# Modulation vectors of a two-block transformer: weights made the stationary operand, in plain f32

## What is computed

```python
mod = jax.nn.silu(c) @ w_mod[l] + b_mod[l]
sh1, sc1, gt1, sh2, sc2, gt2 = jnp.split(mod[:, None, :], N_MOD, axis=-1)
mod_c = jax.nn.silu(c_ctx) @ w_mod[l] + b_mod[l]
h_lat = modulate_2(x, norm1_g[l], sh1, sc1)
h_ctx = modulate_2(ctx, norm1_g[l], csh1, csc1)
```

## Time and profile before

| | us |
|---|---|
| median of 3 runs | 4677.69 |
| lowest, highest run | 4676.04, 4678.01 |
| span of the profiled execution, first to last instruction | 4676.2 |
| from the first load of `w_mod` to the end of the last bias addition, `mod1` | 8.68 to 95.62 |
| the same for `mod2` | 2651.00 to 2735.62 |
| TensorE matmuls, share of the span | 74% |
| TensorE weight loads, share of the span | 59% |
| mean granted TensorE clock, share of 2.4 GHz | 0.878 |

### The profile page before, as it was taken

How to read it: one execution, slowest core, us unless ns; L and a number is a source line. 1 busy time by engine, 2 the same in 40 slices (tenths; PEclk the granted TensorE clock), 3 DMA queues, 4 the chain that set the end, 5 groups by cost and what they waited for, 6 DMA issues and landing times. The chain is left out here.

```text
span 4676.2 us, 54928 instructions
## 1 busy us (share of the span) xinstructions
PE 3468.8 (74%) x18716; PEld 2774.4 (59%) x18716; DVE 2909.6 (62%) x4362; ACT 1528.0 (33%) x1968; POOL 1362.9 (29%) x512
## 2 busy tenths in 40 slices
PE   6683767876777777777777676877676987877968
PEld 3473537865565666666656345757355865766856
DVE  5224647773799998999999645349747823144441
ACT  5110421112355555555555431112013521212121
POOL 0020000001255555655555202115320033333423
PEclk9895888967899999999999888887788998988989
DMA  6110000000587887887887531000010022222322
GB/s 250 50 61 9 5 25 1 1 15 23 214 296 270 299 295 273 297 294 273 298 296 281 190 117 50 35 26 1 0 45 7 1 72 72 73 71 77 98 66 74
DMA packets 136745, 573.07 MB, mean 123 GB/s; under 512 B 12977, under 2 KB 17457, under 8 KB 103729
## 3 DMA queue, kind: packets, MB, share of 16 engines
q1 hardware_dynamic: 136528, 570.21, 34.4%
HBM read 568.07 MB, written 2.10 MB: 122 GB/s over the span
## 5 line engine op out<-in xcount | busy, mean ns | idle before, releaser
L1841 POOL TENSOR_TENSOR ex_d_low<-ex_d,ex_d_high 128x1024 fp32r<-128x1024 f32 x256 | 800.3, 3126 | 724.8 <-ACT ex_d_high L1823 724.8
L1770 PE MATMUL psum<-ex_gu_high,ex_xe 128*128 128x256 f32 x2048 | 560.0, 308 | 371.6 <-DVE ex_gu_low L1876 367.3
L1770 PEld LDWEIGHTS psum<-ex_gu_high,ex_xe 128*128 128x128 f32 x2048 | 417.2, 204 | 497.5 <-DVE ex_gu_low L1876 424.2
L1876 DVE TENSOR_TENSOR ex_gu_low<-ex_gu,ex_gu_high 128x2048 fp32r<-128x2048 f32 x256 | 620.5, 2424 | 63.0 <-ACT ex_gu_high L1812 51.3
L1770 PE MATMUL psum<-ex_gu_low,ex_xe 128*128 128x256 f32 x2048 | 535.0, 295 | 0.0
L1812 ACT CAST ex_gu_high<-ex_gu 128x2048 fp32r<-128x2048 f32 x256 | 486.7, 1901 | 9.7 <-DMA ex_gu<-in_w_gate_up 5.8
L1770 PEld LDWEIGHTS psum<-ex_gu_low,ex_xe 128*128 128x128 f32 x2048 | 418.7, 204 | 0.9
L1892 DVE CAST ex_hT<-ex_hid 128x64 fp32r<-128x64 f32 x256 | 400.8, 1565 | 8.9
L466 POOL TENSOR_TENSOR out_w_low<-out_w,out_w_high 128x1024 fp32r<-128x1024 f32 x16 | 39.3, 2463 | 786.6 <-ACT out_w_high L431 786.6
L1823 ACT CAST ex_d_high<-ex_d 128x1024 fp32r<-128x1024 f32 x256 | 266.1, 1040 | 2.7 <-PE psum L1794 2.4
L1794 PE MATMUL psum<-ex_d_high,ex_hT 128*128 128x512 f32 x512 | 229.7, 449 | 12.4 <-POOL ex_d_low L1841 9.8
(11 more groups left out here) (552 smaller groups left out, 8331.0 us busy)
## 6 DMA issues: line engine op xcount, KB each, us to landing
ex_gu<-in_w_gate_up SPq DMA_DIRECT2D x256, 1024.0 KB, 6.6
ex_d<-in_w_down SPq DMA_DIRECT2D x256, 512.0 KB, 5.7
mod_w<-in_w_mod SPq DMA_DIRECT2D x24, 2048.0 KB, 9.2
ff_up_w<-in_w_up SPq DMA_DIRECT2D x44, 512.0 KB, 3.5
ff_down_w<-in_w_down SPq DMA_DIRECT2D x16, 704.0 KB, 4.0
out_w<-in_w_out SPq DMA_DIRECT2D x16, 512.0 KB, 3.4
in2x_w<-in_w_in_x SPq DMA_DIRECT2D x16, 512.0 KB, 3.2
in2z_w<-in_w_in_z SPq DMA_DIRECT2D x16, 512.0 KB, 3.3
```

The lines of the kernel that those rows point to most:

```text
L1770: ins = pe.matmul(k.bank(c % 2, 2 * P), xe[:, (c // NCH) % 2, t, :, :].rearrange("p a c -> p (a c)"), w, start=t == 0 and p_ == 0, stop=t ...
L1841: pool.tensor_tensor(dw_lo[:, q % 2, :], dw[:, b, :], dw_hi[:, q % 2, :], ALU.subtract).then_inc(s["down_low"], 1)
L1876: v.tensor_tensor(gu_lo[:, c % 2, :, :], gu[:, b, :, :], gu_hi[:, c % 2, :, :], ALU.subtract).then_inc(s["up_low"], 1)
```

## The change

The vectors become the moving operand and the weights the stationary one. The host lays the matrix out in tiles of 128 x 128. A piece is now 4 column tiles of 8 row tiles each, in one contiguous run of 16 KB for each partition, again 2 MB, and there are again 12 pieces. They go to a ring of four buffers. For each column tile 8 plain f32 matmuls (stationary 128 x 128 of weights, moving 128 x 2 of the SiLU of the conditions) add up two columns of PSUM; the results of all 48 column tiles lie in one bank, and one VectorE instruction adds the bias to all of them at the end. The split into high and low parts, the copy of rows and the turning matmuls go. SyncE asks for piece n+4 when the matmuls of piece n are done.

```diff
-        with nc.Block() as block:
-            @block.sync
-            def _(sp):
-                with sp.Fori(0, turns) as i:
-                    for j in range(B):
-                        sp.wait_ge(s["low"], i * B + j + 1)
-                        sp.dma_start(wbuf[j][:, :, :], w[:, bass.ds((i * B + j) * N, N)].rearrange(
-                            "(k p) n -> p k n", p=P)).then_inc(loaded[j], 16)
...
+    nc, RING, PER = k.nc, 4, 4
+    CHUNKS = 6 * D // P // PER
+    loaded = [k.sem(f"{name}_w_loaded{b}") for b in range(RING)]
+    used = k.sem(f"{name}_w_used")
+    with ExitStack() as tmp:
+        ring = k.sb(f"{name}_w", [P, RING, PER, KT, P], tmp)
         with nc.Block() as block:
             @block.sync
             def _(sp):
+                for n in range(CHUNKS):
+                    if n >= RING:
+                        sp.wait_ge(used, n - RING + 1)
+                    sp.dma_start(ring[:, n % RING, :, :, :].rearrange("p c t m -> p (c t m)"),
+                                 w[n, :, :]).then_inc(loaded[n % RING], 16)
 
             @block.tensor
             def _(pe):
+                pe.wait_ge(k.conditions_ready, 1)
+                for n in range(CHUNKS):
+                    pe.wait_ge(loaded[n % RING], 16 * (n // RING) + 16)
+                    for c in range(PER):
+                        at = 2 * (n * PER + c)
                         for t in range(KT):
+                            ins = pe.matmul(k.psum[:, 0, at:at + 2], ring[:, n % RING, c, t, :],
+                                            k.silu_c[:, stream:stream + 2, t], start=t == 0, stop=t == KT - 1)
+                    ins.then_inc(used, 1)
 
             @block.vector
             def _(v):
+                v.wait_ge(used, CHUNKS)
+                v.tensor_tensor(mod[:, :, :], k.bank(0, 2 * CHUNKS * PER).rearrange("p (c s) -> p c s", s=2),
+                                bias.unsqueeze(2).to_broadcast([P, CHUNKS * PER, 2]), ALU.add)
...
+    fours = lambda w: np.ascontiguousarray(tiled(w).reshape(12, 4, P, KT, P).transpose(0, 2, 1, 3, 4)).reshape(12, P, 4096)
+    out["w_mod"], out["w_mod_2"] = fours(g["w_mod"][0]), fours(g["w_mod_2"][0])
```

More of the change, by code:

```diff
@@ L177, in modulation @@
 def modulation(k, name, w, stream, bias, mod):
[L182 to L187, removed]
-    with ExitStack() as tmp:
[L189 to L194, removed]
+    nc, RING, PER = k.nc, 4, 4
+    CHUNKS = 6 * D // P // PER
+    loaded = [k.sem(f"{name}_w_loaded{b}") for b in range(RING)]
+    used = k.sem(f"{name}_w_used")
+    with ExitStack() as tmp:
+        ring = k.sb(f"{name}_w", [P, RING, PER, KT, P], tmp)
         with nc.Block() as block:
@@ L204, in _ @@
             @block.tensor
             def _(pe):
[L206 to L214, removed]
-                        for t in range(KT):
[L216 to L247, removed]
+                pe.wait_ge(k.conditions_ready, 1)
@@ L249, in _ @@
             @block.vector
             def _(v):
[L251 to L270, removed]
@@ L272, in _ @@
-                positions(v, turns, B, LEAD, position)
+                v.wait_ge(used, CHUNKS)
+                v.tensor_tensor(mod[:, :, :], k.bank(0, 2 * CHUNKS * PER).rearrange("p (c s) -> p c s", s=2),
+                                bias.unsqueeze(2).to_broadcast([P, CHUNKS * PER, 2]), ALU.add)
 def norm_modulate(k, name, streams, bank0=0):
@@ L2541, in second_layout @@
                                                        (6720, 8768)))
-    out["w_mod_2"] = g["w_mod_2"][0]
     out["w_in_z2"], out["w_in_q2"], out["w_in_k2"], out["w_in_g2"] = tiled(z), tiled(q), tiled(kk), tiled(gates)
```

## The result

The changed kernel takes **4853.61 us** (median of 5 runs, 4848.12 to 4855.91), against 4677.69 us for the kernel before (5 runs beside it). The ratio is 1.0375, with a 95% interval of 1.0362 to 1.0387. It is slower by 176 us; 174.4 us and 4852 us were forecast, within 4838 to 4870. The profiled execution has a span of 4846.3 us, 7 us under the median of the runs.

The account below looks back on a forecast made before the run. The prediction took the weight transfers, 5.45 us per 2 MB piece, to bound both calls. TensorE's pairs at 0.213 us would add 86.6 and 87.8 us: 4676.2 + 174.4 = 4850.6 us span, median 4852, range 4838 to 4870.

Parts of the forecast that it names:

- The number of pairs: TensorE in each modulation call: 384 plain f32 matmuls, two load-and-matmul records each, so 768 pairs, 64 for a piece.
- The price of a pair: TensorE's weight load plus short matmul: 0.213 us at the low clock, taken from the router and L718; about 0.11 after dense matmuls.
- Which clock: TensorE in both calls: clock stays at 0.50 (1.2 GHz), so all 768 pairs cost 0.213 us.
- The sum for a call: First landing, 163.8 us of pairs, 0.27 and 0.26 us for VectorE: +86.6 us in `mod1`, +87.8 in `mod2`.
- The first landing: Arrival of each call's first piece: taken as unchanged; at most 2.6 us a call better or 1.2 us worse.
- the straight line: VectorE's one 96-column instruction: 0.26 us, between 0.17 us for 8 columns and 0.417 us for 256.
- fetching the unrolled code: Instruction fetch for the 384 unrolled matmuls: an allowance of 0 to 8 us for both calls.
- Rival 1: TensorE's clock comes up in both calls: pairs at 0.1115 us, +18.6 us, 4696 us; chance 0.06.
- Rival 2: Transfers stay the bound in both calls if a pair costs under 0.085 us: -22 us, 4655 us; chance 0.02.
- Rival 3: Dearer TensorE pairs, from waiting short matmuls or code fetch: at 0.25 us +57 more, 4909 us; chance 0.03.
- the transfers set the pace, 5.45 us for 2 MB: Both calls of the kernel before: DMA engines full, a piece every 5.45 us, no compute engine full.

Follow-up runs that it names:

- experiment 1: Changed kernel with 128 moving columns (126 of them ones) in place of 2: 4699.75 us, ratio 1.005 to the kernel before.
- experiment 5: Changed kernel with 128 moving columns for the first 6 pieces of a call and 2 for the last 6: 4771.21 us, ratio 1.0199.
- experiment 2: Changed kernel with 64 moving columns in place of 2: 4848.64 us, ratio 1.0368.
- experiment 4: Kernel before with only the contiguous layout (2 MB pieces, 16 KB runs a partition), arithmetic and ring of three kept: 4680.57 us, ratio 1.001.
- experiment 7: Kernel before with 24 contiguous pieces of 1 MB in four sets of buffers, in place of 12 of 2 MB in three: 4666.36 us, ratio 0.9981.
- experiment 8: Kernel before with 24 contiguous pieces of 1 MB in six sets of buffers, turned columns in the rows' PSUM bank: 4662.58 us, ratio 0.9968.
- experiment 9: Kernel before's arithmetic with 24 pieces of 1 MB in six sets of buffers, old layout (1 KB runs): 4676.42 us, ratio 1.0.
- experiment 10: Experiment 8 again (24 contiguous 1 MB pieces, six sets of buffers), on the same chip as experiment 9: 4660.61 us, ratio 0.9964.

## Why the prediction was right

- **The number of pairs**, 768 for a call: on record as forecast, x1536.
- **The price of a pair**, 0.213 us: 0.213 us. Both rows on which it stood had the clock at 0.50, and so had the new call. Experiments 1 and 5 show that it is the clock and not the tile: 0.112 us at 1.00, the other price of that part.
- **Which clock**: at 0.50 throughout `mod2`. This was the step with the largest lever, 156 us between the two prices, and it was chosen by what rows of the same kind did: L718 and the router stayed low, L1614 did not. That 27 us of such rows would hold for 164 us was an extrapolation, and it held. Experiments 1 and 2 repeat both outcomes in this very place.
- **The sum for a call**: +86.6 and +87.8 were forecast, +86.0 and +88.0 came, counted from the first load. The first landing, taken as unchanged, was 8.65 us after the issue in `mod1` (9.21 before) and 8.3 us in `mod2` (8.0 before), well inside the bounds. `mod1` began 1.3 us later, since the conditions did; VectorE's instruction took the 0.26 us of the straight line. No gap was seen for fetching the unrolled code, for which 0 to 8 us were allowed without a run behind it; `mod1` and `mod2` each show 768 pairs without a break. In this execution the rest of the kernel was some 5 us shorter, which explains its span of 4846.3 against 4850.6 us; nothing in the change bears on it, and no run here shows a cause. The medians differ by 175.9 us. That the median came within 2 us of the forecast is in part luck: single runs of the changed kernel spread over 7.8 us.
- **Rival 1**, the raised clock, was priced at +18.6 us (4696); experiment 1 raised it and measured +24.0 us (4699.75). The 4.0 and 6.0 us at the low level at the start of its calls, which the price left out, cost 1.9 and 2.9 us of that, worked out from the two prices of a pair. The rule of the Trainium skill, "TensorE: Matmul & The Clock Gate", section "LDWEIGHTS (loading the stationary operand)", on a load of 128 columns holds at the high level, 0.112 us against 0.107, and not at the low one, 0.213 us.
- **Rival 2**, the transfers as the bound, needed a pair under 0.1 us. None was seen even with the clock up.
- **Rival 3**, dearer pairs, did not come: in experiment 5 matmuls of 2 columns were 0.112 us apart at the high level, no further than those of 128 columns in experiment 1.

One step was too simple without harm to the sum: "the transfers set the pace, 5.45 us for 2 MB". That was the spacing of the first three pieces. Over the call it was 5.79 us, and experiment 4 showed that quicker transfers alone do not shorten it. The ring of three, which waits for VectorE, had its part in it, as far as experiments 4 and 7 to 9 tell. Had a faster form been forecast, this reading would have mispriced it; the same slip made experiment 4's expectation wrong by some 10 us.

## What to carry to other kernels

Price a weight load by the clock that the engine will have in that stretch, and look for rows with as little streaming for each load to tell which clock that is: here the same load cost 0.112 or 0.213 us, and the casts and subtractions that were taken away had mostly been hidden behind transfers. A full share on the DMA engines is not yet a bound in GB/s: look at the whole row of landings and at what the ring waits for, since the first pieces of a ring show the transfer, and the later ones the cycle. Of the two wide and narrow forms the one that makes TensorE do more per load (64 times the columns) was the cheaper here, but at 4700 us it is still slower than the kernel before. Better was the old form with 24 contiguous pieces of 1 MB in six buffers, 4661 to 4663 us against 4677.

## What the runs showed of the hardware

- With back-to-back plain f32 loads of 128 x 128, TensorE's clock stayed at 1.2 GHz for 164 us with 2 and with 64 moving columns for a load, and stood at 2.4 GHz with 128, from 4.0 and 6.0 us after the start of the two calls on. After wide matmuls it stayed up for the first 4.5 us of narrow ones, in both calls, and then fell, with no idle time between (experiment 5).
- In stretches of 8 us and more, a share of 1.00 to 1.09 on the DMA engines went with 348 GB/s for runs of 1 KB (experiment 9), 367 to 389 GB/s for runs of 2 KB (the kernel before) and 397 to 430 GB/s for runs of 8 and 16 KB (the changed kernel, experiments 1, 4, 5, 7, 8 and 10). The share isn't proportional to the rate: with 16 KB runs in a ring of three (experiment 4, 30 to 70 us) it was 0.96 at 364 GB/s.
